# Six transformer layers in one kernel: modulation rows summed on VectorE with the multiply-adds of the start, the scale part placed inside the out-projection, and the first two blocks of a layer taking high parts ahead of low parts

## What is computed

```python
# for each of the layers 0 to 3; c is one vector of 1024, the same for all tokens
ada = silu(c) @ ada_w[L] + ada_b[L]          # (1, 1024) @ (1024, 3072): parts shift, scale, gate
shift, scale, gate = split(ada, 3)
h = rmsnorm(x, norm_g[L]) * (1 + scale) + shift
x = x + gate * mixer(h)                      # mixer: h @ w_in, attention, (o * silu(gate)) @ w_out
# layers 4 and 5: x = x + mixer_2(rmsnorm_2(x, norm_w_2[l]))
```

## Time and profile before

| | |
|---|---|
| median of 3 runs | 2753.47 us (2751.24 to 2755.43) |
| the profiled execution | 2746.99 us, of which the span of the trace is 2745.2 us |
| PE busy | 2406.8 us, 88% |
| DVE busy | 1591.6 us, 58% |
| POOL busy | 910.1 us, 33% |
| ACT busy | 766.2 us, 28% |
| DMA queues | SyncE's 156.33 MB, POOL's 41.95 MB |
| mean granted TensorE clock | 0.919 of full speed |

### The profile page before, as it was taken

One profiled execution on the slowest core, in us unless ns is written; L12 is line 12 of the kernel. 1 busy time (PEld: TensorE's weight loads), 2 busy tenths in 40 slices (PEclk: granted clock), 3 DMA queues, 4 the chain that ended last, 5 costly groups with the idle time before them and its releaser, 6 DMA issues.

```text
span 2745.2 us, 31261 instructions
## 1 busy us (share of the span) xinstructions
PE 2406.8 (88%) x12233; PEld 1831.3 (67%) x12233; DVE 1591.6 (58%) x2435; ACT 766.2 (28%) x1706; POOL 910.1 (33%) x944
## 2 busy tenths in 40 slices
PE   3968898689999899799879989899799998999978
PEld 2756676468887666676666857476477785747656
DVE  7676684753244665565654457683745536766463
ACT  2233212512001453324322152322311215232311
POOL 2873897378601346852020010400302001030120
PEclk7979898888689899899989989999999999999999
DMA  6440455044543001330111202021121120212111
GB/s 211 136 132 9 115 138 123 1 123 116 137 74 62 17 2 40 116 114 32 62 51 57 69 28 76 29 93 46 46 92 62 62 78 31 62 31 78 61 46 62
DMA packets 229157, 200.27 MB, mean 73 GB/s; under 512 B 86835, under 2 KB 213139, under 8 KB 228755
## 3 DMA queue, kind: packets, MB, share of 16 engines
q1 hardware_dynamic: 217491, 156.33, 20.6%
q0 software_dynamic: 11520, 41.95, 5.3%
HBM read 196.16 MB, written 2.10 MB: 72 GB/s over the span
## 4 chain that ended last, share of the span: by engine, by line
PE 60%; POOL 17%; DVE 14%; ACT 5%; issue 3%; DMA 0%; SPq 0%; DVEq 0%; ACTq 0%; POOLq 0%
PE bank L506 14%; PE bank L507 14%; PE bank L508 14%; POOL mix L2198 6%; POOL mix L2195 4%; PE bank L618 4%; PE bank L654 3%; DVE wring_parts L1496 2%; PE bank L632 2%; POOL mix L2201 2%; POOL mix L2182 2%; PE bank L818 1%; DVE bank L1567 1%; DVE whi_parts L1495 1%; PE bank L572 1%
## 5 line engine op out<-in xcount | busy, mean ns | idle before, releaser
L507 PE MATMUL bank<-h_parts,whi_parts 128*128 128x512 f32 (+2 forms) x1336 | 539.1, 404 | 0.0
L1496 DVE TENSOR_TENSOR wring_parts<-wring,whi_parts 128x2048 fp32r<-128x2048 f32 (+1 forms) x138 | 330.1, 2392 | 4.8
L1495 DVE CAST whi_parts<-wring 128x2048 fp32r<-128x2048 f32 (+1 forms) x138 | 195.1, 1414 | 196.8 <-PE bank L508 158.4
L507 PEld LDWEIGHTS bank<-h_parts,whi_parts 128*128 128x128 f32 (+2 forms) x1336 | 253.8, 190 | 69.9 <-issue 6.0
L2198 POOL TENSOR_TENSOR mix<-mix 128x512 f32<-128x512 f32 (+1 forms) x160 | 216.3, 1352 | 12.5
L506 PE MATMUL bank<-vt_parts,whi_parts 128*128 128x512 f32 (+2 forms) x472 | 199.6, 423 | 18.0 <-POOL h_parts L2229 12.1
L507 PE MATMUL bank<-mix_parts,whi_parts 128*128 128x512 f32 x512 | 204.1, 399 | 0.0
L506 PE MATMUL bank<-pt_parts,whi_parts 128*128 128x512 f32 x392 | 165.5, 422 | 31.1 <-DVE wring_parts L1496 16.2
L508 PE MATMUL bank<-vt_parts,wring_parts 128*128 128x512 f32 (+2 forms) x472 | 190.5, 404 | 0.0
L1567 DVE CUSTOM_DVE_ANT_0 bank<-bank,causal 128x128 f32<-128x128 f32 (+3 forms) x256 | 120.3, 512 | 75.5 <-PE bank L618 75.1
L2195 POOL TENSOR_TENSOR mix<-mix,cond 128x1024 f32<-128x1024 f32 x80 | 161.0, 2013 | 8.7 <-DMA mix<-in_ada_w 7.0
(11 more groups left out here) (372 smaller groups left out, 5347.5 us busy)
## 6 DMA issues: line engine op xcount, KB each, us to landing
wring<-in_w_in SPq DMA_DIRECT2D x60, 1024.0 KB, 5.2
mix<-in_ada_w POOLq DMA_DIRECT2D x80, 512.0 KB, 4.8
wring<-in_w_out SPq DMA_DIRECT2D x16, 1024.0 KB, 5.2
wring<-in_mla_w_in SPq DMA_DIRECT2D x10, 1024.0 KB, 7.1
wring<-in_mla_w_out SPq DMA_DIRECT2D x8, 1024.0 KB, 5.4
wring<-in_swa_w_in SPq DMA_DIRECT2D x32, 256.0 KB, 4.8
wring<-in_nsa_w_in SPq DMA_DIRECT2D x32, 256.0 KB, 4.6
wring<-in_nsa_w_in SPq DMA_DIRECT2D x6, 1024.0 KB, 6.0
```

The source lines that it names most:

```text
L507: pe.matmul(bank, lh, rl, start=False, stop=False)
L1495: chain(dve.tensor_copy(high, whole))
L1496: dve.tensor_tensor(low, whole, high.bitcast(F32), ALU.subtract).then_inc(done, 1)
```

## The change

Four things. (1) POOL's tree is gone. POOL only issues the loads (`ada_loads`), now of two row chunks by 512 columns, and DVE weights and sums them with one multiply-add per row chunk (`ada_rows`), in pieces of 2 to 4 between its other work: 32 rows in the in-projections of layers 0, 1 and 2, 16 in that of layer 3, and 16 in the out-projections of layers 0, 1 and 2. (2) The scale part of the next layer is summed over partitions inside the out-projection, ahead of its fourth unit. (3) `tables(1)` moves behind the `prepare` of `kv_b`. (4) `first_blocks` multiplies the high part of a chunk (two matmuls for each block) as soon as ACT has it, and takes the low part two chunks later.

```diff
@@ -517,12 +520,22 @@
             def first_blocks(keys, slots):
                 b = [open_bank(A, key) for key in keys]
-                for k in range(KC):
-                    right = hk(k)
-                    for j in range(2):
-                        mm = product(b[j][:, :], [t[:, k, j * P:(j + 1) * P] for t in by_chunk(slots)], right, k == 0, k == KC - 1)
-                        if k == KC - 1:
-                            mm.then_inc(A.full, 1)
+                unseen[0] = 0
+                for step in range(KC + LOW_LAG):
+                    if step < KC:
+                        pe.wait_ge(*cnt(h_kept))
+                        for j in range(2):
+                            high, low = [t[:, step, j * P:(j + 1) * P] for t in by_chunk(slots)]
+                            pe.matmul(b[j][:, :], high, hh[step], start=(step == 0), stop=False)
+                            pe.matmul(b[j][:, :], low, hh[step], start=False, stop=False)
+                    k = step - LOW_LAG
+                    if k >= 0:
+                        pe.wait_ge(*cnt(h_ready))
+                        for j in range(2):
+                            high = by_chunk(slots)[0][:, k, j * P:(j + 1) * P]
+                            mm = pe.matmul(b[j][:, :], high, h_parts[:, k, :], start=False, stop=(k == KC - 1))
+                            if k == KC - 1:
+                                mm.then_inc(A.full, 1)
             unseen = [0]
@@ -586,7 +599,7 @@
                 n = 3 * L + part
-                pe.wait_ge(*(cnt(start_summed, 2) if n < 2 else cnt(ada_summed)))
+                pe.wait_ge(*(cnt(start_summed, 2) if n < 2 else (ada_step, 2 * KC * (n - 1))))
                 bank = open_bank(V, ("ada", L, part))
                 for j in range(8):
                     mm = pe.matmul(bank[:, j:j + 1], acc[:, n % 2, j * P:(j + 1) * P], ones[:, 0:1], start=True, stop=True)
@@ -656,6 +669,8 @@
             def out_proj(L, n_k, between=None, midway=None):
                 for i in range(4):
+                    if L + 1 < len(LAYERS) and i == 3:
+                        modulation(L + 1, 1)
                     keys = [(L, "y", 2 * i + j) for j in range(2)]
                     b = [open_bank(V, key) for key in keys] if n_k == 2 else None
                     for k in range(n_k):
@@ -895,8 +910,6 @@
-                if L + 1 < len(LAYERS):
-                    modulation(L + 1, 1)
@@ -1633,6 +1646,26 @@
                     g = COLS["norm_g"][0] + 8 * L
                     chain(dve.scalar_tensor_tensor(out=to, in0=to, scalar=1.0, in1=cols[:, g:g + 8], op0=ALU.add, op1=ALU.mult))
+            summed = [0]
+            def ada_rows(more):
+                for _ in range(more):
+                    n, at = divmod(summed[0], 2 * KC)
+                    half, k = divmod(at, KC)
+                    u, n = KC * (n + 2) + at // 2, n + 2
+                    summed[0] += 1
+                    if k % 2 == 0:
+                        dve.wait_ge(ada_loaded[u % 2], 16 * (u // 2 + 1 - KC))
+                    t = ada_ring[:, u % 2, S * (k % 2):S * (k % 2 + 1)]
+                    to = acc[:, n % 2, S * half:S * (half + 1)]
+                    if k == 0:
+                        dve.wait_ge(*V.filled(("ada",) + todo[n - 2]))
+                        dve.tensor_scalar(to, t, cond[:, 0:1], None, ALU.mult).then_inc(ada_step, 1)
+                    else:
+                        dve.scalar_tensor_tensor(out=to, in0=t, scalar=cond[:, k:k + 1], in1=to, op0=ALU.mult, op1=ALU.add).then_inc(ada_step, 1)
+                    dve.wait_ge(*cnt(ada_step))
             def tables(source):
                 ang, turns, less = tmp[:, :], rs[:, :], raw[:, 0, 4:]
@@ -1671,7 +1704,6 @@
-                tables(1)
@@ -1739,6 +1771,7 @@
                               pt_parts[:, 1, (t - 1) % 3, :], lat_split)
                     for b in range(KC):
                         gate((L, "gate", b), mix[:, b, :])
+                        ada_rows(2 if L else 4)
                         if b == 1 and L:
                             rope((L, "kpe"))
                         if b % 2:
@@ -1747,6 +1780,7 @@
                         constants()
                     prepare()
                     if L == 0:
+                        tables(1)
                         dve.wait_ge(*cnt(tables_act, 3))
                         rope((L, "kpe"))
                     for b in range(4):
@@ -1765,12 +1799,14 @@
                 elif kind == "swa":
                     for b in range(8):
                         rope((L, "q", b), scale)
+                        ada_rows(2)
                         if b % 2:
                             prepare()
                     rope((L, "k", 0))
                     prepare()
                     for b in range(KC):
                         gate((L, "gate", b), mix[:, b, :])
+                        ada_rows(2)
                         if b in (1, 3):
                             prepare()
@@ -1863,15 +1901,17 @@
                         got = dve.tensor_scalar(lamt[:, e:e + 1], invsel[:, 0:1], -LOG_G[e], None, ALU.mult)
                     got.then_inc(decay_rel, 1)
                 for b in range(KC):
+                    if b == 6 and L + 1 < len(LAYERS):
+                        modulation(L + 1, 1)
                     residual(L, b)
                     if b:
                         add_square(L + 1, b - 1)
                     if b % 2 and b < KC - 1:
                         prepare()
+                    if b < 5 and L + 1 < len(LAYERS):
+                        ada_rows(3 if b < 4 else 4)
                 add_square(L + 1, KC - 1)
                 prepare()
-                if L + 1 < len(LAYERS):
-                    modulation(L + 1, 1)
             norm_apply(4, lambda k: col("final_norm_g", k), x, x_normed)
             dve.wait_ge(*cnt(x_normed, KC))
             for k in range(KC):
@@ -2171,38 +2211,18 @@
             pool.wait_ge(*cnt(const_step))
             pool.iota(pcol[:, :], [[0, 1]], base=0, channel_multiplier=1).then_inc(consts_ready, 1)
-            todo = [(L, part) for L in range(len(LAYERS)) for part in range(3)]
-            parts_done = []
-            def ada_load(n, r):
-                L, part = todo[n]
-                u = KC * n + r
-                w = a["ada_w"][L].rearrange("(k p) n -> p k n", p=P)
-                c = part * D + r * P
-                pool.dma_start(ada_ring[:, u % 2, :].rearrange("p (k n) -> p k n", k=KC), w[:, :, c:c + P]).then_inc(ada_loaded[u % 2], 16)
-            def modulation(n):
-                if n == 2:
-                    ada_load(2, 0)
-                    ada_load(2, 1)
-                    pool.wait_ge(*cnt(cond_ready))
-                pool.wait_ge(*V.filled(("ada",) + todo[n - 2]))
-                for r in range(KC):
-                    u = KC * n + r
-                    t = ada_ring[:, u % 2, :].rearrange("p (k n) -> p k n", k=KC)
-                    pool.wait_ge(ada_loaded[u % 2], 16 * (u // 2 + 1 - KC))
-                    pool.tensor_tensor(t, t, cond[:, :, None].to_broadcast([P, KC, P]), ALU.mult).then_inc(ada_step, 1)
-                    for width in (4, 2):
-                        pool.wait_ge(*cnt(ada_step))
-                        pool.tensor_tensor(t[:, 0:width], t[:, 0:width], t[:, width:2 * width], ALU.add).then_inc(ada_step, 1)
-                    pool.wait_ge(*cnt(ada_step))
-                    last = ada_summed if r == KC - 1 else ada_step
-                    pool.tensor_tensor(acc[:, n % 2, r * P:(r + 1) * P], t[:, 0], t[:, 1], ALU.add).then_inc(last, 1)
-                    pool.wait_ge(*cnt(last))
-                    nn, rr = (n, r + 2) if r < KC - 2 else (n + 1, r + 2 - KC)
-                    if nn < len(todo):
-                        ada_load(nn, rr)
+            asked = [2 * KC]
+            def ada_loads(n, ahead):
+                for u in range(asked[0], min(KC * n + ahead, KC * len(todo))):
+                    L, part = todo[u // KC]
+                    w = a["ada_w"][L].rearrange("(k p) n -> p k n", p=P)
+                    k, c = 2 * (u % 4), part * D + S * (u % KC // 4)
+                    if u >= 2 * KC + 2:
+                        pool.wait_ge(ada_step, 2 * (u - 2 * KC - 1))
+                    pool.dma_start(ada_ring[:, u % 2, :].rearrange("p (k n) -> p k n", k=2), w[:, k:k + 2, c:c + S]).then_inc(ada_loaded[u % 2], 16)
+                    asked[0] = u + 1
             def normalise(L):
@@ -2230,9 +2250,7 @@
             for L in STACK_1:
                 low_parts(L)
-                modulation(3 * L + 2)
-                if L + 1 < len(LAYERS):
-                    modulation(3 * L + 3)
+                ada_loads(3 * L + 4, 2)
                 if LAYERS[L] == "nsa":
                     pool.wait_ge(*cnt(gate_sig))
                     for i in range(NT):
@@ -2242,8 +2260,7 @@
                         pool.wait_ge(*cnt(pool_step))
```

(3 more changed lines are left out.)

4 lines of the change are left out of this document (3 added, 1 removed).

## The result

| | before | changed |
|---|---|---|
| median of 4 runs each | 2754.02 us | 2734.12 us |
| lowest to highest | 2751.24 to 2755.43 | 2731.37 to 2738.31 |
| profiled execution, its span | 2746.99, 2745.2 | 2738.31, 2736.6 |
| ratio of the medians, 95% interval | | 0.993 (0.9918 to 0.9943) |

The change makes the kernel faster by 20 us, 0.7%. The forecast was 2703.5 us in a range of 2685 to 2727: the sign was right, the size was not, and the time lies outside the range. It is the time of rival (a), 2732, and the experiments have to say whether for (a)'s reason. The profiled execution after is the slowest of its four, and that of the kernel before is 4 us faster than any of its four, so the two profiles lie only 8.6 us apart.

A forecast was written before the change was run, and what follows sets the result against it. PE, busy 88%, was taken as losing time in waits for POOL's sums, POOL's low parts and DVE's weights. Terms 12 + 7 + 13.5 + 9.5 - 6 + 6 + 8 = 50 gave a median of 2703.5 us, range 2685 to 2727.

The forecast's parts named there:

- rival (a): DVE, not POOL, holds PE, with out-projections late at each unit: gain only 21, median 2732; chance 0.19.
- The out-projections: Out-projections and ends of layers 0 to 2: modulation waits go, DVE rows just fit PE's units; gain 13.5 us.
- L: Load ring: time from DVE's last row to the next landing, taken as 5.2 us; up to 6.7 free in out-projections.
- Layer 2: Rows ahead of the compressed scores' maxima and at the end cost 4.7 us in three places; with slow restarts, loss of 6.
- Layer 0: In-projection up to the scores: DVE becomes the bound, scores at about 183 us; 15 reckoned, gain of 12 taken.
- Attention in layer 0: Attention and out-projection of layer 0 approach layer 3's time without POOL's sums: gain 7 of 8.3 us.
- Layer 1: Ahead of attention, the 8.82 us modulation wait goes and matmuls run warmer; DVE's last rows cost about 2: gain 9.5.
- High parts first: First blocks of a layer: PE starts 1.9 us sooner; five layers at 1.6 give 8 us, layer 0's counted inside its own sum.
- Rival (d): High parts bring nothing because low parts set the unit's end: minus 8, median 2711; chance pooled with the main forecast, 0.62.
- (b): Slower: the loads starve DVE at the ring; 2780 or more at a 12 us turnaround; chance 0.04 of over 2753.
- (c): More comes back: PE stays warm through layer 0's short gaps; gain 66, median 2687; chance 0.12.
- Layer 3: The 5.21 us wait goes since POOL no longer slows DVE; with the slow restart, gain 6 us.

The follow-up runs named there:

- e6: Changed kernel, but six of the eight loads behind each out-projection's rows left out, so DVE sums what stands in the ring: 2710.02 us.
- e9: Changed kernel with the out-projection's 16 rows on DVE as 4, 4, 4, 4 behind the first four residuals, not 3, 3, 3, 3, 4 behind five: 2712.05 us.
- e2: Changed kernel with layer 2's eight weighting operations on POOL put between the loads, not behind the last: 2727.46 us.
- e11: e10 with more of layer 2's rows ahead of the compressed scores (three per rope, then 2, 2, 2, 2, 0, 0, 0, 0 at the gates): 2694.28 us.
- e1: Changed kernel with the scale part's matmuls and their DVE work put back behind the out-projection: 2703.10 us.
- e10: e3 with rows at the gates of layers 1 and 2 as 3, 3, 3, 3, 2, 2, 0, 0, not two each: 2694.79 and 2693.47 us.
- e7: e1 with the first two blocks of a layer as before the change, so without high parts first: 2714.46 us.
- e3: Changed kernel with both edits, scale part behind the out-projection and layer 2's weighting between POOL's loads: 2697.48 us.

## Why the prediction was wrong

**The out-projections: the step that failed.** The sum had "DVE some 0.9 us late", and "PE's 8 matmuls, which take 1.8 (warm)". That is 2.7 us per layer. Measured in the two profiles: 3.3 to 4.4 of wait, 2.7 to 3.4 for the matmuls, and 2.0 to 2.9 for a fourth unit at a lower clock, 9.5 in layer 0. The last term was in no step, though the text itself says that PE starts again slowly. Over three layers that is 20 us of the 34 to 41 us by which the profiles missed the sum. The stage's row in the table shows 14 to 16, since the forecast had put 4 us of layer 0's out-projection under attention.

**Why DVE was late.** The forecast compared DVE's work with PE's per unit (11.1 of 11.2 us) and the ring over the whole out-projection ("L up to 6.7 is free"). Each held by itself. Neither asked when the last rows stand in DVE's order. Four of them are behind the fifth residual, which needs half of the third unit, and PE wants their sum at the third unit's end, 5.6 us later. DVE then has a residual, a square and four rows to do, 0.75 + 0.68 + 3.1 = 4.5, which leaves 1.1 us. It came to that residual at 288.68, some 2.4 us after its bank was full (291.9 - 5.6 = 286.3), 2.0 of it from the first two landings, and lost 2.0 more to the next two. e6 takes the landings away, e9 the placement; either edit alone brings the wait under 0.5 us and, by the medians, 27 us back. L itself was as taken: the loads landed in a median of 4.4 us, and in layer 0 the first turn of the ring was 5.2 us from DVE's last row to its next.

POOL's issue instruction took 0.72 us in the median, and 1.10 us in just those 17 of 80 that began inside DVE's CAST of a unit (848.83 above is one). Each of the 17 ended 0.14 to 0.15 us behind the end of that CAST. The Trainium skill ("SBUF — State Buffer", the warning on DVE blocking DMA) says that POOL cannot write descriptors while DVE runs a copy in a two-port mode, and the ends of these 17 agree with that. The 3.1 us that the Trainium skill gives beside a copy (the same page, "A bandwidth-pool intuition that's wrong") did not come here: what was left of the 1.22 us CAST lengthened the issue by 0.4 us only. The forecast had set the block aside with the reading that DVE was casting beside the issues all the time. In the kernel before that was so for 5 of 80 issues, and these took 1.26 to 1.36 us against 0.92.

**Rival (a)** gave the right time, and half of its reason: DVE holds PE in the out-projection, but at one place per layer and not at each unit. With the placement mended the same DVE work is nearly hidden (e9), so it is not DVE's fullness by itself that cost 20 us, though a DVE filled to 11.1 of 11.2 us could not catch up the 2.0 us of landings.

**Layer 2: the second failed step.** "Three such places cost 4.7" was right for the compressed scores (4.07 us in place of 2.34, and 1.97 at the next) and for the rows at the end (1.88). Missing was what is queued behind POOL's own waits: its loads now wait for DVE, and the weighting stood behind them. e2 shows this to be 5 us of the stage, in a total that is 8.8 us lower by the medians and 3.2 by the profiles. The same text had named the weighting as one that waits for DVE's rows, but not that it does so through POOL's queue. The rest of layer 2, some 10 us instead of 6, is three waits with a slow restart each. It was not taken apart further: e11 moved rows away from the maxima, and 5.10 us of wait stayed.

**Layer 0** came as worked out up to `kv_b`. The first gate was at 97.21 us, the waits of PE at the gate units 1.45, 3.26 and 1.04 us, the tables ended at 166.5 and PE was back at 168.95. Scores came at 187.2 us and not at 183: from there to the first modulation part it was 13.3 us where about 11 were taken, and from that to the first score 4.9 us where 3.6 stood. The gain is 10.8 where 12 was taken and 15 reckoned. PE's 5.27 us at `kv_b` are for ACT and the tables, also as described. **Attention in layer 0** gave 1 us either way and not 3: POOL's sums are gone, and it is still 3 to 5 us longer than the 65.6 of layer 3 in the kernel before, which the forecast took as its measure. Why is open. The other 4 of the 7 us are real, and appear in e1, whose out-projection of layer 0 takes 45.0 us where the kernel before took 49.2.

**Layer 1** gained 7.6 us ahead of attention and not 9.5, and attention took 0.2 to 2.1 us more. Its rows behind the last gate cost the 3 us that were set aside for them: e10 moves them and gets 2.9 back. The rest was not taken apart.

**High parts first** was right, 10.6 us by e7 against e1 with 8 in the sum plus 2 in layer 0. Rival (d) is wrong. Rivals (b) and (c) did not come. One price in (b) is too low by its own terms: L = 7.7 would cost 9 us in the out-projections and, with 3 to 4 us for each of 2.5 us, another 9 in layer 0, 18 and not 13.

**Layer 3** gained 7.0 us ahead of attention where 6 were forecast, and its attention lost 3.2 of them, at a granted clock of 0.95 (1.00 before):

```profile
1241.24:1310.06 68.82, 62.57 (x417) 0.95 0.04 12
```

Its instructions are the same. In e3 the same stretch takes 65.6 us at 1.00. Why the clock falls in some of these kernels and not in others is open.

**The sum.** e3, with both steps mended, is 54.4 us below the kernel before by the medians and 47.4 by the profiles, close to the 50 that was forecast. That is in part luck, as the last column of the table shows. The out-projections and turns gained 32.0 us and not 18.3, or 22.3 with layer 0's 4 us, since the scale part now costs nothing. Layer 2 still lost 15.1 and not 6, and layer 1 gained 5.7 and not 9.5. These misses cancel.

## What to carry to other kernels

- When a sum of work fits into a unit, also write down the last item that a consumer needs, where it stands in its producer's order, and what that place waits for. Here 12 of 16 rows were early and four were late.
- Moving work out of the end of a stage gains only if the end is where it costs. The eight small matmuls of the scale part were free at the end of the out-projection, where PE had a wait anyway. Ahead of the fourth unit they cost some 2 us with their input ready (e9, layer 2), 3.9 with a wait of 0.37 us (e9, layer 0), and 8.6 to 10.0 with a wait of 3.3 to 3.7.
- An engine that issues loads into a ring waits for the ring's consumer. Everything behind those loads in its program waits too, so put its own computation between the loads in the order in which inputs come.
